# A two-layer hybrid trunk with mixture of experts on one core: a fourth 64-slot expert item, state-space input products over a 96-row stack, and a first-phase ring of six slots

## The chip, the cores and the metric

The kernel runs on 1 core of one Trainium2 chip. The metric is the device time of one execution in microseconds (us), lower is better. Five engines work side by side: TensorE (PE, with its weight loads as PEld), VectorE (DVE), ScalarE (ACT), GpSimd (POOL) and SyncE (SP), which here only issues the weight transfers. Each runs its own instructions in order and meets the others at semaphores.

## The reference: what is computed

256 tokens of width 1024 pass two layers. Each layer is a mixer and a feed-forward part; the first feed-forward is dense, the second a mixture of 8 experts with the best 2 per token. All weights are float32.

```python
def hybrid_mixer(xn, ...):
    q, k, v, u_ssm, h_conv, b_gate, c_gate, gate_logits = jnp.split(xn @ w_in, IN_SPLITS, axis=-1)
    y_a = stick_breaking_attention(q, k, v) @ w_br_a
    y_b = s5_ssm(u_ssm, ...) @ w_br_b
    y_c = short_conv(h_conv, b_gate, c_gate, conv_w) @ w_br_c
    merged = g[:, :, 0] * y_a + g[:, :, 1] * y_b + g[:, :, 2] * y_c      # g = sigmoid(gate_logits)
    return merged @ w_out
# in s5_ssm: 16 groups of 16 channels and 64 states
    bu_re = jnp.einsum('gph,blgh->blgp', bb_re, ug)
    bu_im = jnp.einsum('gph,blgh->blgp', bb_im, ug)
# the second feed-forward
    for e in range(N_EXPERTS):
        out = out + combine[..., e:e + 1] * swiglu(xn, w_gate[e], w_up[e], w_down[e])
```

Each expert has three matrices of 1024 x 3584, so the expert weights are 8 x 3 x 1024 x 3584 x 4 bytes = 352.3 MB. With the inputs that are timed, the experts 0 to 7 get 73, 59, 72, 59, 67, 72, 58 and 52 tokens.

## The kernel before

**The first phase** is both mixers and the dense feed-forward. Its weights come as units of 1 MB, in the order of the list `STREAM`, into `ring`, which has `RING` = 7 slots: unit n goes to slot n % RING. A mixer's units are q0, q1, k0, k1, v0, v1, u0, h0, b0, c0, four units gC0 to gC3, gA0, the two units brA0 and brA1, gA1 to gA3, gB0 to gB3 and wo0 to wo3; each gA unit feeds two gate steps, so steps gA6 and gA7 use unit gA3. SP issues the loads in this order (L631). Before unit n it waits until the slot is free. For most units that is when the unit n - RING has been split. The units brA are used raw, and SP waits for the end of their last user, the PE step gA7:

```python
                    old_l, old = STREAM[n - RING]
                    if old[:2] == "br":
                        sp.wait_ge(work_done, Group((old_l, "g" + old[2], KT - 1)).done)
                    else:
                        sp.wait_ge(lo_ready, SPLIT.index((old_l, old)) + 1)
```

**The split.** A unit is cut into a high part (ACT, rounded to float32r, L1235) and a low part (DVE, L1501) in `parts`, which has three places. PE multiplies three pairs of parts, each in one pass (L752), where a float32 product takes more passes. ACT and DVE split a unit when they come to the step that is `AHEAD` = 3 units before its use: the first of the two steps of a unit calls `splits.upto`, ahead of that step's own work. So at step gA6 both engines first split gB1, then do gA6.

**The order of work** on each engine is the list `STEPS`, in which the steps of attention (z, softplus, tail, attend), of the convolution (h, b, c), of the state space (bbT, u, eight steps bu, two steps ys, gelu, glu) and of the gates (gC, gA, gB) are interleaved by hand. Three banks of PSUM (`work`) go round: PE begins a group only when the bank's reader three groups before is done. A step bu multiplies 32 rows of `bbT` by 32 rows of `uT` in float32, twice (L873). Between gA7 and gB0 stands glu, whose PE product needs the output of ACT's gelu. ACT and DVE do gelu right behind gA6 and before gA7.

**The expert phase.** Items of work are (expert, slots). A full item has 96 slots (3 groups of 32), a short one 64; `FEW_AT` names the short ones, 1, 4 and 7, which go to the experts with the fewest tokens. PE's products have a stationary operand of 32 slots, four side by side (L1141 for gate and up, L1159 for down), so an item's PE time follows its groups, while its weights are always 44 MB. The weights stream through `moe_ring`, 34,816 floats per partition in the place of ring, br_slot, parts, hs and xs (17.8 MB), each load waiting (L647) until PE has used what lay there.

## Time and profile before

| what | value |
|---|---|
| three runs | 1540.42, 1537.77, 1540.18 us; median 1540.18 |
| profiled execution, its own time | 1538.63 us |
| its span, first to last instruction | 1536.9 us |
| outside the span | 1.73 us |
| busy: PE, DVE, ACT, POOL | 1502.9, 599.6, 347.7, 219.5 us |
| moved from memory | 462 MB |
| mean granted clock | 0.994 |

The three runs spread over 2.65 us (0.17%). The table's busy times are over the whole span; the phases have different limits, and what an edit is worth has to be read in its own phase.

### The profile page before, as it was taken

The page shows a single profiled execution, that of the slowest core. Times are in us where ns is not written, and L with a number is a line of the kernel's source. Part 1 is how long each engine was busy: PE and PEld are TensorE (multiplying, and loading weights), DVE is VectorE, ACT ScalarE, POOL GpSimd, SP SyncE. Part 2 cuts the span into 40 slices and gives each one's busy share as a digit, 9 for nine tenths or more (in the row PEclk, how much of TensorE's full clock was granted, in tenths as well). Part 3 has the DMA queues.
Part 4 walks back from the last instruction along what each step waited for, and adds up shares of the span by engine and source line. Part 5 has one row for each costly group of instructions (what it writes and reads, how often), then busy time and mean ns, then how long its engine had stood idle before and what let it go on. Part 6 is the DMA issues. An engine that isn't in the chain of part 4 may idle for free.

```text
span 1536.9 us, 30324 instructions
## 1 busy us (share of the span) xinstructions
PE 1502.9 (98%) x13463; PEld 922.1 (60%) x13463; DVE 599.6 (39%) x925; ACT 347.7 (23%) x427; POOL 219.5 (14%) x283
## 2 busy tenths in 40 slices
PE   7999999999999999999999999999999999999997
PEld 6988999999999988994333333333333323333331
DVE  6888667755556477564111211211202012011021
ACT  5443355444445453331000000000000000000001
POOL 3447369300000137200000000000000000000000
PEclk9999999999999999999999999999999999999998
DMA  9732395554554522589999999999999999999995
GB/s 275 234 110 83 116 282 166 191 192 165 192 192 151 174 88 83 165 325 385 372 392 419 419 419 419 419 419 420 419 419 420 420 418 419 419 419 420 419 419 222
DMA packets 146339, 465.00 MB, mean 303 GB/s; under 512 B 10144, under 2 KB 92064, under 8 KB 131872
## 3 DMA queue, kind: packets, MB, share of 16 engines
q1 hardware_dynamic: 143296, 461.40, 77.7%
q8 instruction: 106, 1.74, 0.5%
q0 software_dynamic: 416, 1.05, 0.3%
q10 hardware_dynamic: 2496, 0.61, 0.3%
q14 instruction: 25, 0.20, 0.0%
HBM read 461.98 MB, written 1.05 MB: 301 GB/s over the span
## 4 chain that ended last, share of the span: by engine, by line
PE 59%; DMA 5%; SPq 3%; ACT 1%; DVE 1%; issue 0%; POOL 0%; DVEq 0%; ACTq 0%; POOLq 0%
PE work L1141 14%; PE acc L1159 13%; PE work L752 11%; PE acc L1141 11%; PE ssm_y L1141 4%; SPq L647 3%; DMA moe_ring<-in_moe_w_down 2%; DMA moe_ring<-in_moe_w_gate 2%; DMA moe_ring<-in_moe_w_up 2%; PE acc L1096 1%; PE acc L1109 1%; PE work L873 0%; PE acc L752 0%; PE acc L843 0%; PE work L779 0%
## 5 line engine op out<-in xcount | busy, mean ns | idle before, releaser
L752 PE MATMUL work<-xs,parts 128*128 128x256 f32 x3600 | 455.3, 287 | 9.7 <-DVE xs L1508 4.8
L752 PEld LDWEIGHTS work<-xs,parts 128*128 128x128 f32 x3600 | 442.2, 193 | 19.7 <-issue 15.7
L1141 PE MATMUL work<-moe_ring,arena 128*32 128x448 f32 x2688 | 276.1, 539 | 0.1
L1501 DVE TENSOR_TENSOR parts<-ring,parts 128x2048 fp32r<-128x2048 f32 x94 | 220.0, 2345 | 121.8 <-ACT parts L1235 121.7
L1159 PE MATMUL acc<-moe_ring,arena 128*32 128x512 f32 x2352 | 257.6, 593 | 8.6 <-DMA moe_ring<-in_moe_w_down 7.0
L1141 PE MATMUL acc<-moe_ring,arena 128*32 128x448 f32 x2048 | 216.5, 540 | 1.0 <-ACT arena L1421 0.8
L1235 ACT ACTIVATE parts<-ring 128x2048 fp32r<-128x2048 f32 x94 | 178.7, 1907 | 89.3 <-PE work L752 62.6
L1159 PEld LDWEIGHTS acc<-moe_ring,arena 128*32 128x32 f32 x2352 | 75.8, 110 | 186.2 <-issue 167.9
L1141 PEld LDWEIGHTS work<-moe_ring,arena 128*32 128x32 f32 x2688 | 87.3, 110 | 165.7 <-issue 160.7
L1908 DVE TENSOR_TENSOR arena<-arena,work 128x448 f32<-128x448 f32 x42 | 23.7, 616 | 347.9 <-ACT arena L1421 347.9
L1421 ACT ACTIVATE arena<-acc 128x448 f32<-128x448 f32 x32 | 15.7, 541 | 633.5 <-PE work L1141 633.5
L1141 PEld LDWEIGHTS acc<-moe_ring,arena 128*32 128x32 f32 x2048 | 64.0, 110 | 129.7 <-issue 123.4
L752 PE MATMUL acc<-hs,parts 128*128 128x256 f32 x672 | 83.0, 283 | 1.0 <-DVE hs L1733 1.0
L752 PEld LDWEIGHTS acc<-hs,parts 128*128 128x128 f32 x672 | 81.6, 192 | 1.1 <-DVE parts L1501 1.1
L1141 PE MATMUL ssm_y<-moe_ring,arena 128*32 128x448 f32 x640 | 74.8, 539 | 0.0
L1892 DVE SCALAR_TENSOR_TENSOR arena<-acc,arena 128x512 f32<-128x512 f32 x28 | 21.0, 751 | 108.8 <-PE acc L1096 107.3
L2004 POOL TENSOR_SCALAR_AFFINE_SELECT arena<-arena 128x512 f32<-128x512 f32 x16 | 19.6, 1227 | 296.7 <-DVE arena L1640 273.4
L1341 ACT ACTIVATE sig<-work 128x256 f32<-128x256 f32 x48 | 18.4, 383 | 123.3 <-PE work L752 123.3
L1917 DVE STREAM_TRANSPOSE arena<-acc 128x768 f32<-128x768 f32 x8 | 7.9, 983 | 97.1 <-PE acc L1114 97.1
L1141 PEld LDWEIGHTS ssm_y<-moe_ring,arena 128*32 128x32 f32 x640 | 20.9, 110 | 39.2 <-issue 39.2
L1931 DVE TENSOR_TENSOR arena<-arena,acc 64x512 f32<-64x512 f32 x5 | 3.4, 679 | 92.7 <-ACT arena L1439 92.7
L2092 POOL TENSOR_TENSOR arena<-arena 128x256 f32<-128x256 f32 x16 | 31.2, 1947 | 45.0 <-DVE arena L1676 45.0
(312 smaller groups left out, 1060.3 us busy)
## 6 DMA issues: line engine op xcount, KB each, us to landing
moe_ring<-in_moe_w_gate SPq DMA_DIRECT2D x128, 896.0 KB, 23.8
moe_ring<-in_moe_w_up SPq DMA_DIRECT2D x128, 896.0 KB, 23.7
moe_ring<-in_moe_w_down SPq DMA_DIRECT2D x112, 1024.0 KB, 25.2
ring<-in_w_in SPq DMA_DIRECT2D x44, 1024.0 KB, 6.5
ring<-in_dense_w_gate SPq DMA_DIRECT2D x14, 1024.0 KB, 5.3
ring<-in_dense_w_up SPq DMA_DIRECT2D x14, 1024.0 KB, 5.1
ring<-in_dense_w_down SPq DMA_DIRECT2D x14, 1024.0 KB, 4.9
ring<-in_w_out SPq DMA_DIRECT2D x8, 1024.0 KB, 13.0
```

The lines of the kernel that those rows point to most:

```text
L647: sp.dma_start(moe_view(n, u), w).then_inc(moe_full[sem_of(n, u)], 16)
L752: last = nc.tensor.matmul(out_ap, a, b, start=start and n == 0, stop=stop and n == len(pairs) - 1, skip_group_check=shared)
L1141: last = nc.tensor.matmul(banks[g][GRP * q:GRP * q + GRP, 0:CHUNK], x, w[:, q * CHUNK:q * CHUNK + CHUNK], start=k == 0, stop=k == KT - 1, ...
L1159: last = nc.tensor.matmul(acc[GRP * q:GRP * q + GRP, b, :], eh[:, which, 2 * u + kk, g * GRP:g * GRP + GRP], w[:, kk, half * OUT_COLS:half ...
L1235: nc.scalar.activation(parts[:, s % PARTS, 0, :], ring[:, n % RING, :], ACT.Copy)\
L1341: nc.scalar.activation(sig[:, n % 2, :], bank[:, 0:L], ACT.Sigmoid).then_inc(sig_ready, 1)
L1421: nc.scalar.activation(esilu[:, g, :], gate_banks[g][:, 0:CHUNK], ACT.Silu).then_inc(silu_set, 1)
L1501: tt(parts[:, s % PARTS, 1, :], ring[:, n % RING, :], parts[:, s % PARTS, 0, :].bitcast(F32), ALU.subtract).then_inc(lo_ready, 1)
L1892: stt(h_tok[:, t, lo:lo + OUT_COLS], acc[:, half, :], own_share[:, t:t + 1], h_tok[:, t, lo:lo + OUT_COLS], ALU.mult, ALU.add).then_inc(ad ...
L1908: tt(erow[:, g * CHUNK:(g + 1) * CHUNK], esilu[:, g, :], up_banks[g][:, 0:CHUNK], ALU.mult)\
L2004: last = nc.gpsimd.affine_select(out=blk, in_=blk, compare_op=ALU.is_gt, fill=0.0, base=0, pattern=[[0, HB], [1, P]], channel_multiplier=-1)
L2092: tt(rtmp[:, 0, :], s_re, cosT[:, t, :], ALU.mult)
```

## The change

There are three edits. `FEW_AT` gets a fourth short item, now 1, 3, 5 and 7. The ring of the first phase loses one slot. In the slot's place stands `b_stack`: `bb` and `u` are each cut into a high and a low part, twelve small transfers each per layer stack them in 96 rows (high, high, low against high, low, high), and one float32r product over 96 rows replaces the float32 product over 32. Parts lie in the buffers of h and b of the convolution (`b_high`, `b_low`), in `u_high` (in bbT's place) and in `sig` (`u_low`), so ACT waits for the transfers before it writes there. The first loads of the expert weights are ordered by when their place comes free.

```diff
-    FEW_AT = (1, 4, NE - 1)
+    FEW_AT = (1, 3, 5, NE - 1)
...
-    RING = 7
+    RING = 6
     PARTS = 3
+    STACK = 3
     BR_AT = RING * UW
-    PARTS_AT = BR_AT + UW
+    BB_AT = BR_AT + UW
+    PARTS_AT = BB_AT + UW
...
+            b_stack = before_experts.enter_context(nc.sbuf_tensor("b_stack", [P, SJ, 2, P], F32R))
...
-        bbT = sb("bbT", [P, 4, P])
+        u_high = sb("u_high", [P, CT * L])
...
+        STACKED = 16 * STACK * (P // 32)
...
+            def stack_b(l):
+                sp.wait_ge(b_low_ready, l + 1)
+                for block, part in enumerate((b_high, b_high, b_low)):
+                    for m in range(P // 32):
+                        to = b_stack[rows_of(block), :, :, :].rearrange("r (a m) c n -> r m a (c n)", m=P // 32)
+                        sp.dma_start(to[:, m, :, :].bitcast(F32),
+                                     part[rows_of(m), :].rearrange("r (a n) -> r a n", n=2 * P)).then_inc(b_stacked, 16)
...
             for n, (l, name) in enumerate(STREAM):
                 if n == 1:
                     sp.wait_ge(params_loaded, 16 * PARAMS)
+                if n - RING == STREAM.index((l, "u0")) + 1:
+                    stack_b(l)
+                if n - RING == STREAM.index((l, "u0")) + 3:
+                    stack_u(l)
...
-            for s in range(5):
-                first_of_ring(s)
...
+            for s in sorted(range(FIRST_TURN), key=lambda s: (free_after(s)[-1][0], s)):
+                for _, signal, value in free_after(s):
+                    sp.wait_ge(signal, value)
                 load_unit(*UNITS[s], 0, True)
...
                     elif kind == "bu":
                         if t == 0:
-                            pe.wait_ge(bbT_ready, l + 1)
-                            pe.wait_ge(u_ready, l + 1)
-                        a, b = t // 4, 32 * (t % 4)
+                            pe.wait_ge(b_stacked, STACKED * (l + 1))
+                            pe.wait_ge(u_stacked, STACKED * (l + 1))
                         for q in range(2):
-                            last = nc.tensor.matmul(bank[:, q * L:q * L + L], bbT[b:b + 32, 2 * q + a, :],
-                                                    uT[b:b + 32, a, :], start=True, stop=True)
+                            last = nc.tensor.matmul(bank[:, q * L:q * L + L], b_stack[0:32 * STACK, t, q, :],
+                                                    u_stack[0:32 * STACK, t, :], start=True, stop=True)
...
                     elif kind in ("h", "b"):
                         bank = arrived(Group((l, kind, t)))
+                        act.wait_ge(b_stacked, STACKED * (l + 1))
...
                     elif kind == "bbT":
                         bank = arrived(Group((l, kind, t)))
-                        nc.scalar.activation(bbT[:, :, :].rearrange("p t n -> p (t n)"), bank[:, :], ACT.Copy)\
-                            .then_inc(bbT_ready, 1)
+                        nc.scalar.activation(b_high.bitcast(F32R), bank[:, :], ACT.Copy).then_inc(b_high_ready, 1)
+                    elif kind == "u":
+                        bank = arrived(Group((l, kind, t)))
+                        nc.scalar.activation(u_high[:, :].bitcast(F32R), bank[:, :], ACT.Copy).then_inc(u_high_ready, 1)
...
+                        dve.wait_ge(u_high_ready, l + 1)
+                        tt(u_low.bitcast(F32R), bank[:, :], u_high[:, :], ALU.subtract).then_inc(u_low_ready, 1)
...
+                    elif kind == "bbT":
+                        bank = arrived(Group((l, kind, t)))
+                        dve.wait_ge(b_high_ready, l + 1)
+                        tt(b_low.bitcast(F32R), bank[:, :], b_high, ALU.subtract).then_inc(b_low_ready, 1)
```

SP's instructions in the first mixer, before the change. The names are buffer, source and shape; in brackets stand the semaphores that SP waits for (`lo_ready` counts split units, `work_done` PE's finished groups).

```order
L618 DMA br_slot<-in_w_br_c 128x2x1024
L631 DMA ring<-in_w_in 128x8x256 [waits lo_ready] x5
L631 DMA ring<-in_w_br_a 128x2x1024 [waits lo_ready] x2
L631 DMA ring<-in_w_in 128x8x256 [waits lo_ready] x3
L618 DMA br_slot<-in_w_br_b 128x2x1024 [waits work_done]
L631 DMA ring<-in_w_in 128x8x256 [waits lo_ready] x2
L631 DMA ring<-in_w_in 128x8x256 [waits work_done] x2
L631 DMA ring<-in_w_out 128x8x256 [waits lo_ready] x4
```

The same place on SP with the change:

```order
L654 DMA br_slot<-in_w_br_c 128x2x1024
L667 DMA ring<-in_w_in 128x8x256 [waits lo_ready] x3
L630 DMA b_stack<-arena 32x2x256 [waits b_low_ready]
L630 DMA b_stack<-arena 32x2x256 x11
L667 DMA ring<-in_w_in 128x8x256 [waits lo_ready] x2
L638 DMA hs<-u_high 32x2x256 [waits u_low_ready]
...
L667 DMA ring<-in_w_br_a 128x2x1024 [waits lo_ready] x2
L667 DMA ring<-in_w_in 128x8x256 [waits lo_ready] x3
L654 DMA br_slot<-in_w_br_b 128x2x1024 [waits work_done]
L667 DMA ring<-in_w_in 128x8x256 [waits lo_ready]
L667 DMA ring<-in_w_in 128x8x256 [waits work_done] x2
L667 DMA ring<-in_w_in 128x8x256 [waits lo_ready]
```

Behind the load of w_br_b stood two loads (gB0, gB1) that wait for a split and then two (gB2, gB3) that wait for PE's gA7. With six slots only gB0 is left ahead of that wait, and the two behind it are gB1 and gB2.

ACT's instructions around gelu in the first mixer, before the change. An ACTIVATE into `parts` is the high half of a split, with the slot of the ring that it reads; `sig` is a gate step; L1326 is gelu.

```order
L1341 ACTIVATE sig<-work 128x256 [waits gate_used,work_done] x2
L1235 ACTIVATE parts<-ring 128x2048 [waits work_done,slot_full0]
L1341 ACTIVATE sig<-work 128x256 [waits gate_used,work_done]
L1326 ACT_TABLE_LOAD
L1326 ACTIVATE arena<-arena 128x256 [waits gelu_in] x2
L1341 ACT_TABLE_LOAD [waits gate_used]
L1341 ACTIVATE sig<-work 128x256 [waits work_done]
L1330 ACTIVATE arena<-work 128x512 [waits work_done]
L1235 ACTIVATE parts<-ring 128x2048 [waits work_done,slot_full1]
```

The same place with the change:

```order
L1377 ACTIVATE sig<-work 128x256 [waits gate_used,work_done] x2
L1266 ACTIVATE parts<-ring 128x2048 [waits work_done,slot_full3]
L1377 ACTIVATE sig<-work 128x256 [waits gate_used,work_done]
L1360 ACT_TABLE_LOAD
L1360 ACTIVATE arena<-arena 128x256 [waits gelu_in] x2
L1377 ACT_TABLE_LOAD [waits gate_used]
L1377 ACTIVATE sig<-work 128x256 [waits work_done]
L1364 ACTIVATE arena<-work 128x512 [waits work_done]
L1266 ACTIVATE parts<-ring 128x2048 [waits work_done,slot_full4]
```

The order on ACT stays. The unit whose split stands in front of gA6 and gelu is gB1 both times: number 21 of the stream, in slot 21 % 7 = 0 before and 21 % 6 = 3 now.

## Rows read from the trace of the kernel before

**Rows 1.** The page: busy time, and GB/s in 40 slices of the span.

```profile
PE 1502.9 (98%) x13463; PEld 922.1 (60%) x13463; DVE 599.6 (39%) x925; ACT 347.7 (23%) x427; POOL 219.5 (14%) x283
GB/s 275 234 110 83 116 282 166 191 192 165 192 192 151 174 88 83 165 325 385 372 392 419 419 419 419 419 419 420 419 419 420 420 418 419 419 419 420 419 419 222
```

**Rows 2.** Windows of the expert phase: stretch, busy PE, PEld, DVE, ACT, POOL, clock, DMA, GB/s.

```profile
780.00:800.00 20.00, 20.00 (x200) 6.37 (x196) 3.36 (x11) 0.00 (x0) 0.00 (x0) 1.00 1.01 420
...
1220.00:1240.00 20.00, 17.29 (x164) 4.40 (x156) 4.17 (x4) 1.42 (x3) 0.00 (x0) 1.00 1.01 419
...
1518.00:1521.00 3.00, 2.20 (x20) 0.58 (x24) 0.00 (x0) 0.00 (x0) 0.00 (x0) 1.00 0.47 191
```

**Rows 3.** Instruction groups of PE by line and shape in the expert phase.

```profile
L1141 PE MATMUL work<-moe_ring,arena 128*32 128x448 f32 x2688 | 276.1, 539 | 0.1
L1159 PE MATMUL acc<-moe_ring,arena 128*32 128x512 f32 x2352 | 257.6, 593 | 8.6 <-DMA moe_ring<-in_moe_w_down 7.0 <-DVE arena L1919 1.6
L1141 PE MATMUL acc<-moe_ring,arena 128*32 128x448 f32 x2048 | 216.5, 540 | 1.0 <-ACT arena L1421 0.8 <-DMA moe_ring<-in_moe_w_gate 0.3
L1141 PE MATMUL ssm_y<-moe_ring,arena 128*32 128x448 f32 x640 | 74.8, 539 | 0.0
```

**Rows 4.** Timeline of PE at a step bu: start, length, line, instructions.

```profile
139.99 1.12 PE L873 MATMUL work<-arena,bbT 32*128 32x256 f32 x4
```

**Rows 5.** Timeline of PE at glu, which begins when gA7 ends, first mixer.

```profile
177.05 1.89 PE L752 MATMUL work<-arena,wglu 128*128 128x256 f32 x8
```

**Rows 6.** Timeline of SP: the two loads that wait for gA7, first mixer.

```profile
177.25 0.99 SPq L631 DMA_DIRECT2D ring<-in_w_in  x2
```

**Rows 7.** Timeline of ACT: the split of gB1, gelu, and the split of gB2.

```profile
167.14 1.91 ACT L1235 ACTIVATE parts<-ring 128x2048 fp32r<-128x2048 f32 x1
...
173.38 0.81 ACT L1326 ACTIVATE arena<-arena 128x256 f32<-128x256 f32 x2 [0.23 <-DVE arena L1680]
...
182.53 1.91 ACT L1235 ACTIVATE parts<-ring 128x2048 fp32r<-128x2048 f32 x1 [2.96 <-DMA ring<-in_w_in]
```

**Rows 8.** Timeline of DVE: gA6, gelu's input, and the low part of gB2.

```profile
171.94 0.42 DVE L1691 TENSOR_TENSOR arena<-sig,work 128x256 f32<-128x256 f32 x1 [0.50 <-ACT sig L1341]
...
172.86 0.87 DVE L1680 SCALAR_TENSOR_TENSOR arena<-arena,dskip,ssm_y 128x256 f32<-128x256 f32 x2
...
184.48 2.29 DVE L1501 TENSOR_TENSOR parts<-ring,parts 128x2048 fp32r<-128x2048 f32 x1 [4.11 <-ACT parts L1235]
```

**Rows 9.** PE before and behind its longest wait, and the clock there (timeline, windows).

```profile
43.49 11.68 PE L752 MATMUL work<-parts,xs 128*128 128x256 f32 x96
...
71.55 14.44 PE L752 MATMUL work<-xs,parts 128*128 128x256 f32 x96 [2.69 <-DVE parts L1501]
...
76.00:78.00 2.00, 2.00 (x12) 2.00 (x12) 2.00 (x1) 0.00 (x0) 1.93 (x2) 0.59 0.53 90
```

**Rows 10.** Timeline of ACT and DVE, first mixer: splits, rotation tables, convolution.

```profile
69.40 1.90 ACT L1235 ACTIVATE parts<-ring 128x2048 fp32r<-128x2048 f32 x1
...
69.11 2.29 DVE L1501 TENSOR_TENSOR parts<-ring,parts 128x2048 fp32r<-128x2048 f32 x1
...
78.43 1.65 DVE L1602 TENSOR_TENSOR arena<-arena,power 128x1024 f32<-128x1024 f32 x1
...
81.25 1.23 DVE L1604 TENSOR_TENSOR arena<-arena,power 128x1024 f32<-128x1024 f32 x1
...
86.03 0.69 DVE L1647 TENSOR_TENSOR arena<-work,arena 128x512 f32<-128x512 f32 x1 [0.97 <-PE work L752]
...
89.62 0.69 DVE L1658 TENSOR_TENSOR arena<-arena 128x512 f32<-128x512 f32 x1
```

**Rows 11.** Timeline of PE: the branch product of gC0, and the second tail step.

```profile
92.17 1.03 PE L752 MATMUL work<-arena,br_slot 128*128 128x256 f32 x4
...
115.51 0.91 PE L843 MATMUL acc<-arena,neg_incl 128*128 128x384 f32 x2 [0.29 <-POOL arena L2004]
```

**Rows 12.** The page: SP's smallest transfers, KB each, median us to landing.

```profile
out<-arena SPq DMA_DIRECT2D x4, 256.0 KB, 2.1
```

More of the change, by code:

```diff
@@ L327, in trunk_kernel @@
         x_parts = [xs[:, q * KT * L:(q + 1) * KT * L].rearrange("p (k n) -> p k n", n=L) for q in range(2)]
+        u_stack = hs[:, :].rearrange("p (t n) -> p t n", n=L)
         h_parts = hs[:, :].rearrange("p (b q f n) -> p b q f n", b=2, q=2, n=L)
@@ L386, in trunk_kernel @@
         v_tiles = v[:, :, :].rearrange("p t n -> p (t n)").rearrange("p (t n) -> p t n", n=L)
+        flat_conv = [conv[:, :, :].rearrange("p t n -> p (t n)") for conv in (hconv, bconv)]
+        b_high, b_low = flat_conv
+        u_low = sig[:, :, :].rearrange("p t n -> p (t n)")
         scaled_pair = attn[:, :, :].rearrange("p h n -> p (h n)")[:, 0:4 * L].rearrange("p (b q n) -> p b q n", b=2, q=2)
@@ L606, in _, with rows_of, stack_u @@
                     .then_inc(x_loaded[half], 16)
+            def rows_of(m):
+                return slice(32 * m, 32 * m + 32)
+            def stack_b(l):
[5 more added lines that the diff above has]
+                                     part[rows_of(m), :].rearrange("r (a n) -> r a n", n=2 * P)).then_inc(b_stacked, 16)
+            def stack_u(l):
+                sp.wait_ge(u_low_ready, l + 1)
+                for block, part in enumerate((u_high, u_low, u_high)):
+                    for m in range(P // 32):
+                        to = u_stack[rows_of(block), :, :].rearrange("r (a m) n -> r m a n", m=P // 32)
+                        sp.dma_start(to[:, m, :, :].bitcast(F32),
+                                     part[rows_of(m), :].rearrange("r (a n) -> r a n", n=L)).then_inc(u_stacked, 16)
             for n, (l, name) in enumerate(STREAM):
@@ L657, in load_block, with free_after @@
                 return waited
-            def under(s):
+            def free_after(s):
                 lo, hi = PLACE[UNITS[s]]
-                return range(lo // UW, (hi - 1) // UW + 1)
-            def first_of_ring(s):
-                behind = max(m for m in range(RING) if (len(STREAM) + m) % RING in under(s))
-                sp.wait_ge(lo_ready, S0 + behind - RING + 1)
-                load_unit(*UNITS[s], 0, True)
-            def last_part_under(s):
-                slots = [(at - PARTS_AT // UW) // 2 for at in under(s) if PARTS_AT // UW <= at < HS_AT // UW]
-                return max((n for n in range(S0 - PARTS, S0) if n % PARTS in slots), default=-1)
@@ L672, in _ @@
-            sp.wait_ge(down_banks, KT // 2)
-            in_hs = [s for s in range(FIRST_TURN) if PLACE[UNITS[s]][0] >= HS_AT and PLACE[UNITS[s]][1] <= XS_AT]
-            for s in in_hs:
-                load_unit(*UNITS[s], 0, True)
-            for s in range(5):
-                first_of_ring(s)
-            sp.wait_ge(work_done, Group((DEPTH - 1, "gB", KT - 1)).done)
-            in_br = [s for s in range(FIRST_TURN) if BR_AT <= PLACE[UNITS[s]][0] and PLACE[UNITS[s]][1] <= PARTS_AT]
-            for s in in_br:
-                load_unit(*UNITS[s], 0, True)
@@ L682, in _, with meets @@
-            for s in range(5, HALF_UNITS):
-                first_of_ring(s)
-            for part in range(S0 - PARTS, S0):
-                sp.wait_ge(*used_up(*SPLIT[part]))
-                for s in range(HALF_UNITS, FIRST_TURN):
-                    if s not in in_hs + in_br and part == (
-                            S0 - 1 if PLACE[UNITS[s]][1] > XS_AT else last_part_under(s)):
-                        load_unit(*UNITS[s], 0, True)
+                def meets(start, size):
+                    return lo < start + size and start < hi
@@ new lines, in free_after @@
+                after = []
+                for j in range(RING):
+                    if meets((len(STREAM) - RING + j) % RING * UW, UW):
+                        split_no = S0 - RING + j
+                        after.append((split_no - PARTS + 0.8, lo_ready, split_no + 1))
+                if meets(BR_AT, UW):
+                    after.append((S0 - 5 + 0.1, work_done, Group((DEPTH - 1, "gB", KT - 1)).done))
+                if meets(BB_AT, UW) or meets(HS_AT, XS_AT - HS_AT):
+                    after.append((0, work_done, Group((DEPTH - 1, "bu", SJ - 1)).done))
@@ new lines, in free_after @@
+                for part in range(S0 - PARTS, S0):
+                    if meets(PARTS_AT + part % PARTS * 2 * UW, 2 * UW):
+                        after.append((part + 0.1, *used_up(*SPLIT[part])))
+                if meets(XS_AT, MOE_SIZE - XS_AT):
+                    after.append((S0 - 1 + 0.1, *used_up(*SPLIT[S0 - 1])))
+                return sorted(after, key=lambda entry: entry[0])
+            for s in sorted(range(FIRST_TURN), key=lambda s: (free_after(s)[-1][0], s)):
+                for _, signal, value in free_after(s):
+                    sp.wait_ge(signal, value)
+                load_unit(*UNITS[s], 0, True)
@@ L1333, in _ @@
                         n = gate_number(l, kind[1], t)
+                        if kind == "gC" and t == 0:
+                            act.wait_ge(u_stacked, STACKED * (l + 1))
                         if kind == "gB" and t >= KT - 2:
```

11 lines of the change are left out of this document (8 added, 3 removed).

## The prediction

> **What bounds the kernel now.** I read the page first. PE is busy for 1502.9 of 1536.9 us, and the slices show two regimes of transfer: 83 to 385 GB/s up to slice 20, then 419 or 420 almost to the end [rows 1]. So PE's share alone does not say who sets the end. I looked at each phase for itself.
>
> In the expert phase the windows answer it. From 780 us on the transfers run at 419 or 420 GB/s, whether PE is busy for 20.00 of 20 us or for 17.29 [rows 2]; in slices 19 to 21, which are item 0, they run at 372 to 392 [rows 1]. The weights are 352.3 MB, at 420 GB/s 839 us. PE's products of the phase take 276.1 + 216.5 + 74.8 + 257.6 = 825.0 us [rows 3]. By item: five full items have 3 groups and three short ones 2, together 21, at 825.0 / 21 = 39.3 us; a full item costs PE 118 us, a short one 79, and the transfers of any item 105. PE falls 13 us behind in a full item and makes up 26 in a short one. The ring holds 17.8 MB, 42 us of transfer, and absorbs this. The ring is full only in item 0, where PE sets the pace; behind it the transfers never stop. The expert phase is bound by transfer once item 0 is through.
>
> The first phase is the reverse: PE goes from product to product, and the transfers rest between units. There a microsecond of PE, or of a wait of PE, is a microsecond of the whole, and also of the start of the expert phase.
>
> **The short item.** Item 3 and item 5 become short and item 4 full: one group fewer, 39.3 us less PE work. Item 0 stays full and item 1 short, so the only stretch that PE paces is as it was, and from there on the bytes left and their rate are the same. What hides the edit is the stream itself: PE waits longer for weights. I cost it at 0. The four experts with the fewest tokens outside item 0's have 52, 58, 59 and 59, all within 64 slots, so no ninth item is made. The last item is short as before and PE had caught up there (2.20 busy of 3.00 us at the end, with the clock at 1.00) [rows 2], so the tail stays too.
>
> **The products.** A step bu takes 1.12 us for two float32 products in four records [rows 4]. With float32r parts it is two records at the pace of the other split products, 11.68 us for 96 or 0.12 each [rows 9]; with the tail of the last one 0.32 us, so 0.80 less. That the new ones have 96 rows and not 128 should not make them slower. 16 steps give 16 x 0.80 = 12.8 us. Two of them, bu2 in either layer, give nothing: they stand between z1 and tail1, and PE already waits 0.29 us at tail1 for the chain through ACT, DVE and POOL [rows 11]. That returns 1.6 us. Net -11.2.
>
> **The stacking, first layer.** DVE is the late engine here; PE waits for its split until 71.55 [rows 9]. At 69.11 DVE starts that split [rows 10]; now `b_low` goes first, one operation on 128x512, whose like takes 0.69 us and hides 0.1 of it [rows 10]. PE waits 0.6 us more. Then SP issues twelve copies. Two loads were issued in 0.99 us [rows 6], so twelve take 6.0, and the last lands 2.1 us later if it is like SP's stores [rows 12]: they start at 70.0, and 70.0 + 8.1 = 78.1. ACT sits at its copy of h until then, and behind it are the splits of gC0 (at 69.40 before [rows 10]) and gC1. On DVE follow the low part of gC0, three operations of rotation tables (78.43 to 82.48, 4.1 us), the low part of gC1, and the convolution (86.03 to 90.31, 4.3 us) [rows 10]. Behind 78.1 come 0.5 + 1.9 us on ACT and 2.3 + 4.1 + 2.3 + 4.3 on DVE, less 0.1 at each handover: the convolution is ready at 93.4. PE asks for it at 92.17 + 0.6 [rows 11]: it waits 0.6 us. DVE then runs some 3 us late, and the three banks pass on about 1.5 us of that to PE. Together +2.7. In the second layer there are no tables in the way and nothing is late, so the copies are covered: 0. `stack_u` has more than 10 us of h, b, c and gC0 on PE as its cover in both layers.
>
> Both ends for the copies: 0 below; above, twelve at 2.1 us each one behind the other, 25.2 us, which would make PE wait some 18 us in the first layer and, without the tables, 14 in the second. I take the low end, because SP's own issues are the nearest rows. The Trainium skill speaks against the edit here: "DMA: Bandwidth & Descriptors", section Bandwidth, puts a transfer of 64 KB at 0.95 us and calls those below that size descriptor-dominated. By it twelve copies would take 11.4 us, the total would come to about 1567, and no row here shows such copies on SP.
>
> **The ring of six.** For nearly all units a slot less costs nothing: a load is issued six units ahead of its use and a load lands within 5.3 us (177.25 to 182.53 [rows 6, 7]), while PE spends 5.8 us on a unit of 48 products [rows 9]. One place is different. The units behind brA0 and brA1 in the ring wait not for a split but for PE's gA7. With seven slots these are gB2 and gB3, issued at 177.25, when gA7 has ended at 177.05 [rows 5, 6]; gB2 is first read by ACT at 182.53, after 2.96 us of waiting, and by then gelu is done (173.38 to 174.19) [rows 7] and PE is in the gB steps. With six slots they are gB1 and gB2, and ACT and DVE split gB1 ahead of gA6, where it now happens at 167.14 [rows 7]. PE goes on to the end of gA7. Then glu needs gelu, gelu is behind gA6 on ACT and DVE, and gA6 is behind the split of a unit whose load has just been issued. The chain, with T = 177.05: load seen by ACT at T + 5.5 (182.53 [rows 7]), high part 1.9, low part done at T + 9.7 (184.48 + 2.29 [rows 8]), then gA6's product, its sum and gelu's input, 171.94 to 173.73, 1.8 us [rows 8], and gelu's end 0.46 us behind that (174.19 [rows 7]): T + 11.9. PE had glu at T [rows 5]. It stands idle for 11.9 us in each mixer, 23.8 in all; nothing on PE can cover it, because the products are issued in order.
>
> The clock follows. After 2.69 us of waiting PE ran at the lower level of 1.2 GHz (granted 0.59 as late as 76 to 78 us) and took 14.44 us for 96 products that take 11.68 at full clock [rows 9]: 2.7 us lost. A wait of 11.9 us should cost this again, so 5.4 in two layers; the bounds are 0 and, with the low level for twice as long, 11.
>
> What is late next: the gate steps of ACT behind glu start late, but PE starts glu late by the same amount, and gB2 has landed by then. The first expert loads move with the splits, and as a whole they get more time ahead of PE.
>
> **The sum.** The profiled execution took 1538.63 us: - 11.2 + 2.7 + 23.8 + 5.4 = + 20.7 gives 1559.3. The median of the three runs shown is 1.55 us above the profiled one. I say 1559.
>
> **The rivals.**
> *The wait is hidden and the kernel is faster.* If gB1 were in the ring in time, what is left is - 11.2 + 2.7: 1530. For it speaks only that a slot less is a rare limit elsewhere. It is decided by when gB1 lands: by about 167 us, where ACT splits it now [rows 7], nothing is lost, and each us behind that costs one as soon as gelu's margin of some 3 us is gone. Against it stands the order: the load waits for gA7, the split is ahead of gA6. Chance 0.06.
> *The short item pays.* If PE were the bound throughout, 39.3 us less work would come off: 1559 - 39 = 1520, or about 1540 if half does. For it speaks that PE is busy for 20.00 of 20.00 us in most windows; against it that the transfers stay at 419 GB/s when PE rests [rows 2]. Chance 0.05.
> *The copies are slow.* With 1 us each they end 6 us later, PE waits 6 us more in the first layer and about half as long in the second, where a part is covered: 1568; with 2 us, above 1580. Chance 0.12.
> *The clock falls in the starved items.* Short items would keep PE waiting a quarter of the time. If it then ran at 1.2 GHz, a short item would take 157 us against 105 of transfer, up to 52 us for each of three. Against it: 17.29 of 20 and 2.20 of 3 us busy, both at 1.00 [rows 2]. Chance 0.03.
> The forecast itself gets 0.74.
>
> **How the numbers follow.** The forecast's own range is 1553 to 1566: the stall 10 to 13 us, the clock 0 to 3 a time, the first layer's stacking 0 to 5. The range reaches down to 1550 for a part of the gain in the expert phase and up to 1569 for copies of 1 us. A change below 0.2% (3.1 us) can't be told from none here. Faster holds the first rival and most of the second, 0.10; within 0.2% 0.02; slower 0.88.
>
> **What would show it.** Right: PE idle for about 12 us ahead of glu in each mixer, with ACT waiting for a load of w_in ahead of a split; the granted clock near 0.5 behind it; bu at about 0.26 us; PE busy down by some 50 us to about 1450; transfers still at 419 GB/s and the expert phase, from its first product to the end, as long as before. Wrong: no idle ahead of glu; the expert phase shorter by more than 3 us; `b_stack` copies landing after 80 us in the first layer. The likeliest error of size is the clock's price and the copies; of sign, only the wait for gA7.

## The result, and the profile of the changed kernel

The changed kernel takes 1565.6 us (median of 4 runs, 1564.57 to 1566.6), the kernel before 1539.97 us (4 runs): a ratio of 1.0168, 95% interval 1.0156 to 1.0181. It is 25.6 us slower; the forecast was 1559, 19 slower, with a range up to 1569. The profiled execution took 1565.42 us, its span 1563.6.

The page of the kernel after, which answers to [rows 1]: busy time by engine, the granted clock of PE in 40 slices, and the transfer rate in the same slices.

```profile
PE 1467.7 (94%) x13063; PEld 906.3 (58%) x13063; DVE 606.3 (39%) x927; ACT 346.4 (22%) x426; POOL 214.2 (14%) x283
PEclk9999899999999999899999999999999999999999
GB/s 277 157 197 74 138 189 166 195 165 192 183 189 135 167 225 55 145 233 364 381 370 420 419 419 419 420 419 419 419 420 419 419 420 419 420 419 419 419 420 232
```

PE is busy for 35.2 us less, yet the span is 26.7 us longer: what was saved in work came back as idle time. Its clock dips in slices 4 and 16 (the first is 0), in which the two glu steps lie. The transfers run at 419 or 420 GB/s from slice 21 on, as before.

The waits of the kernel after: engine and line that waited, engine and line that released it, us in total, times, longest.

```profile
ACT parts L1266 <- DMA ring<-in_w_in: 31.8, 2, 15.9
...
PE work L784 <- ACT arena L1360: 24.0, 2, 12.0
```

L1266 is ACT's split, L1360 gelu. Two waits of ACT for a load, two of PE for gelu; neither line had a wait of this size before. The timeline of SP, ACT, DVE and PE (one below the other) shows how they hang together in the first mixer.

```profile
178.61 2.46 SPq L667 DMA_DIRECT2D ring<-in_w_in  x3
...
183.95 1.91 ACT L1266 ACTIVATE parts<-ring 128x2048 fp32r<-128x2048 f32 x1 [15.87 <-DMA ring<-in_w_in]
...
189.59 0.81 ACT L1360 ACTIVATE arena<-arena 128x256 f32<-128x256 f32 x2 [2.16 <-DVE arena L1722]
...
185.96 2.29 DVE L1537 TENSOR_TENSOR parts<-ring,parts 128x2048 fp32r<-128x2048 f32 x1 [16.18 <-ACT parts L1266]
...
189.08 0.87 DVE L1722 SCALAR_TENSOR_TENSOR arena<-arena,dskip,ssm_y 128x256 f32<-128x256 f32 x2
...
176.69 1.89 PE L784 MATMUL work<-arena,ring 128*128 128x256 f32 x8
190.55 3.75 PE L784 MATMUL work<-arena,wglu 128*128 128x256 f32 x8 [11.97 <-ACT arena L1360]
193.74 3.42 PE L784 MATMUL work<-xs,parts 128*128 128x256 f32 x24
```

The rows show a circle in time: PE ends gA7 at 178.6, only then does SP load gB1; ACT has stood at its split of gB1 for 15.87 us, DVE behind ACT for 16.18, and gelu (189.59) is queued on both behind that split. PE, which has nothing but glu next, stands idle for 11.97 us. Then it runs at half speed: glu takes 3.75 us against 1.89 [rows 5]. The windows there (columns as in [rows 2]) show the clock, idle first, then at work:

```profile
182.00:184.00 2.00, 0.00 (x0) 0.00 (x0) 0.00 (x0) 0.05 (x1) 0.00 (x0) 0.98 1.08 364
...
190.00:192.00 2.00, 1.45 (x4) 1.21 (x5) 0.00 (x0) 1.97 (x4) 0.00 (x0) 0.50 1.11 350
...
194.00:196.00 2.00, 2.00 (x17) 1.91 (x16) 0.69 (x1) 1.67 (x2) 0.97 (x1) 0.96 1.10 349
```

PE stopped at 178.6, the granted clock was at 0.50 from 184 on and back at 0.96 in the stretch from 194. In the second mixer the same happens: glu starts at 658.90, behind 11.99 us of idle time.

The second cost is the stacking of the first mixer. The timeline of SP, of ACT, and of PE at the first gC branch (compare [rows 10, 11]):

```profile
71.50 8.96 SPq L630 DMA_DIRECT2D b_stack<-arena  x12
...
81.97 0.60 ACT L1339 ACTIVATE arena<-work 128x512 f32<-128x512 f32 x1 [13.18 <-DMA b_stack<-arena]
...
97.14 1.13 PE L784 MATMUL work<-arena,br_slot 128*128 128x256 f32 x4 [3.76 <-DVE arena L1700]
...
98.36 4.54 PE L784 MATMUL work<-xs,parts 128*128 128x256 f32 x24
```

SP issued the twelve copies in 8.96 us, 0.75 us each. ACT's copy of h waited for them for 13.18 us, the convolution (L1700) was late behind it, PE waited 3.76 us and then ran slowly (4.54 us for 24 products that take 3.04 to 3.14 at full clock). ACT went on at 81.97 us, so the last copy had landed only then: this is one of the prediction's own signs of being wrong, copies into `b_stack` landing after 80 us.

**Where the time stands in all kernels.** The start of a kernel varies from one execution to the next: the first tail step begins between 83.9 and 87.1 us in the twelve traces, in no order that follows the edits. So I read each trace in two stretches: from PE's first tail step to its first expert product, and from there to the end of the span. Each number is the difference of two starts in PE's timeline.

| kernel | first phase, us | against before | expert phase, us | median, us |
|---|---|---|---|---|
| before | 613.6 | | 837.5 | 1540.0 |
| after | 639.2 | +25.7 | 837.5 | 1565.6 |
| e1_order | 613.5 | -0.1 | 837.2 | 1539.3 |
| e2_float32_products | 645.6 | +32.0 | 835.9 | 1570.3 |
| e3_short_items | 613.5 | 0.0 | 836.2 | 1537.2 |
| e4_filled | 633.5 | +19.9 | 836.5 | 1559.2 |
| e5_room | 609.6 | -3.9 | 837.7 | 1534.6 |
| e6_splits_behind | 602.6 | -11.0 | 837.4 | 1528.5 |
| e7_splits_behind_before | 613.9 | +0.3 | 837.1 | 1538.6 |
| e8_later_split | 610.8 | -2.8 | 837.1 | 1536.2 |
| e9_items_back | 602.6 | -10.9 | 838.2 | 1528.0 |
| e10_tail_later | 611.3 | -2.3 | 837.7 | 1534.5 |

The kernel before, run again beside the experiments, had medians of 1538.97 (e1 to e4), 1538.3 (e5 to e8) and 1538.38 us (e9, e10), 1.0 to 1.7 us below the 1539.97 beside the kernel after. Where two runs from different groups are compared below, the stretches of the table or the ratios are the safer numbers. The expert phase is within 1.6 us of the kernel before in every kernel, with three or four short items, begun at 688 or at 733 us, and with either order of the first expert loads. That order, the third edit, was not run by itself. All that follows is about the first phase.

### The profile page after: what moved, and what is told of

It is laid out like the page before. It is cut to its first block, busy times and chain, and to the rows that moved or that the text cites. A ratio compares the mean times of both kernels' runs of the same rounds, so it can differ in the third digit from the quotient of the medians.

```text
span 1563.6 us, 29591 instructions
## 1 busy us (share of the span) xinstructions
PE 1467.7 (94%) x13063; PEld 906.3 (58%) x13063; DVE 606.3 (39%) x927; ACT 346.4 (22%) x426; POOL 214.2 (14%) x283
## 3 DMA queue, kind: packets, MB, share of 16 engines
q0 software_dynamic: 416, 1.05, 0.3%
HBM read 461.98 MB, written 1.05 MB: 296 GB/s over the span
## 4 chain that ended last, share of the span: by engine, by line
PE 41%; DMA 15%; SPq 7%; DVE 2%; POOL 1%; issue 1%; ACT 1%; DVEq 0%; ACTq 0%; POOLq 0%
PE work L1172 10%; PE acc L1190 9%; PE work L784 8%; PE acc L1172 7%; DMA moe_ring<-in_moe_w_down 7%; SPq L683 7%; DMA moe_ring<-in_moe_w_up 5%; DMA moe_ring<-in_moe_w_gate 3%; PE ssm_y L1172 2%; PE acc L1127 1%; PE acc L1140 1%; POOL arena L2134 0%; PE acc L784 0%; DVE parts L1537 0%; DMA ring<-in_w_in 0%
## 5 line engine op out<-in xcount | busy, mean ns | idle before, releaser
L1190 PE MATMUL acc<-moe_ring,arena 128*32 128x512 f32 x2240 | 249.8, 594 | 23.8 <-DMA moe_ring<-in_moe_w_down 22.0
L1172 PE MATMUL work<-moe_ring,arena 128*32 128x448 f32 x2560 | 264.7, 540 | 7.3 <-DMA moe_ring<-in_moe_w_up 7.2
L1266 ACT ACTIVATE parts<-ring 128x2048 fp32r<-128x2048 f32 x94 | 179.0, 1908 | 111.9 <-PE work L784 60.3
L1190 PEld LDWEIGHTS acc<-moe_ring,arena 128*32 128x32 f32 x2240 | 71.6, 110 | 198.4 <-issue 146.9
L1172 PEld LDWEIGHTS work<-moe_ring,arena 128*32 128x32 f32 x2560 | 82.5, 110 | 169.0 <-issue 140.0
L1172 PEld LDWEIGHTS acc<-moe_ring,arena 128*32 128x32 f32 x2048 | 63.4, 110 | 136.0 <-issue 114.2
L1172 PE MATMUL ssm_y<-moe_ring,arena 128*32 128x448 f32 x512 | 60.1, 539 | 0.0
L1172 PEld LDWEIGHTS ssm_y<-moe_ring,arena 128*32 128x32 f32 x512 | 17.2, 110 | 30.9 <-issue 30.9
L1953 DVE STREAM_TRANSPOSE arena<-arena 128x1344 f32<-128x1344 f32 (+1 forms) x16 | 33.7, 2109 | 0.6
## 6 DMA issues: line engine op xcount, KB each, us to landing
moe_ring<-in_moe_w_down SPq DMA_DIRECT2D x112, 1024.0 KB, 25.7
```

The costliest lines, as they stand in the source:

```text
L1172: last = nc.tensor.matmul(banks[g][GRP * q:GRP * q + GRP, 0:CHUNK], x, w[:, q * CHUNK:q * CHUNK + CHUNK], start=k == 0, stop=k == KT - 1, ...
L1190: last = nc.tensor.matmul(acc[GRP * q:GRP * q + GRP, b, :], eh[:, which, 2 * u + kk, g * GRP:g * GRP + GRP], w[:, kk, half * OUT_COLS:half ...
L1266: nc.scalar.activation(parts[:, s % PARTS, 0, :], ring[:, n % RING, :], ACT.Copy)\
L1953: nc.vector.transpose(eh[:, which, :, :].rearrange("p f (g n) -> p f g n", g=NG)[:, :, 0:ng, :], erow[:, :].rearrange("p (g i f) -> p f g ...
```

## The experiments

**The wait for gB1.** In e1_order one line of the order of loads differs from the kernel after; no compute engine has an instruction moved.

```diff
-    + ["gA0"] + [f"brA{n}" for n in range(QW // UC)] + [f"gA{n}" for n in range(1, GU)]
+    + ["gA0", "gA1"] + [f"brA{n}" for n in range(QW // UC)] + [f"gA{n}" for n in range(2, GU)]
```

> The kernel after, with one edit to the order of loads: gA1 stands ahead of brA0 and brA1, so that the two slots that are held until gA7 pass to gB2 and gB3, as they did with seven slots. The instructions of PE, ACT, DVE and POOL are the same. Theory (the wait for gB1 costs the time): both waits of 12.0 us ahead of glu and the slow stretches behind them (1.8 and 1.5 us) go, 27.3 in all: 1565.6 - 27.3 = 1538.3, no idle of PE ahead of glu over 0.5 us. Rival (six slots are too few in general, or brA is now late for gA0): PE waits elsewhere in its place, and the time stays above 1548.

Measured 1539.33 us, ratio to before 1.0003 (0.9993 to 1.0012). No wait ahead of glu is left; 25.7 us of the first phase came back by moving one load. Six slots are enough in this order. That the kernel is no faster than before, though its products are shorter, has its reason in new waits: 3.43 us at the first gC branch (with slow products behind it), 1.0 us more at the second tail step of each mixer, 0.84 us at the first ys step, and 2.56 and 2.58 us at the last ys step. PE's timeline in the second mixer, then POOL's and DVE's beside it:

```profile
622.75 1.89 PE L784 MATMUL work<-arena,ring 128*128 128x256 f32 x8
627.22 1.07 PE L911 MATMUL ssm_y<-arena,cblk 128*32 128x256 f32 x16 [2.58 <-POOL arena L2139]
...
618.34 2.64 POOL L2134 TENSOR_TENSOR arena<-arena 128x256 f32<-128x256 f32 x1 [1.28 <-DVE arena L1718]
620.94 0.92 POOL L2135 TENSOR_TENSOR arena<-arena 128x256 f32<-128x256 f32 x1
621.82 0.96 POOL L2136 TENSOR_TENSOR arena<-arena 128x256 f32<-128x256 f32 x1
622.73 2.77 POOL L2137 TENSOR_TENSOR arena<-arena 128x256 f32<-128x256 f32 x1
...
618.12 2.26 DVE L1537 TENSOR_TENSOR parts<-ring,parts 128x2048 fp32r<-128x2048 f32 x1
...
622.37 2.56 DVE L1537 TENSOR_TENSOR parts<-ring,parts 128x2048 fp32r<-128x2048 f32 x1 [0.19 <-ACT parts L1266]
```

POOL's two long operations begin inside DVE's two splits and end 0.6 us behind them; the same operations beside other work take 0.72 to 1.01 us. In this trace twelve of POOL's 128x256 operations take 2.64 us or more: every one begins inside a split and ends 0.57 to 0.61 us behind its end. A short operation is held in the same way, as POOL's and DVE's rows in the kernel after show (its neighbours of the same shape take 0.20 to 0.27 us):

```profile
239.09 2.17 POOL L2094 TENSOR_TENSOR power<-power 128x8 f32<-128x8 f32 x1
...
238.91 2.29 DVE L1537 TENSOR_TENSOR parts<-ring,parts 128x2048 fp32r<-128x2048 f32 x1 [0.53 <-ACT parts L1266]
```

So what a collision costs POOL is what is left of DVE's split when POOL's operation begins, whatever that operation's own size. The Trainium skill says it of the pair ("GPSIMD Engine Reference", Specifications): POOL's way to SBUF is shared with DVE and contended when DVE reads two inputs from SBUF, as this split does. The trace agrees, at 1.9 and 2.0 us for these two.

In e2_float32_products the state-space products of the kernel before are put back; the ring keeps six slots, and the items and the order of the expert loads stay as in the kernel after.

```diff
-    pe.wait_ge(b_stacked, STACKED * (l + 1))
-    pe.wait_ge(u_stacked, STACKED * (l + 1))
+    pe.wait_ge(bbT_ready, l + 1)
+    pe.wait_ge(u_ready, l + 1)
...
-    b_stack[0:32 * STACK, t, q, :], u_stack[0:32 * STACK, t, :]
+    bbT[b:b + 32, 2 * q + a, :], uT[b:b + 32, a, :]
```

> The kernel after with the state-space products as they were before: float32 products, no split of b and u, no copies; the 2048 floats of b_stack stay unused, so that the ring still has six slots. Theory (ring of six alone makes the loss): 1540.0 + 27.3 = 1567.3, PE idle 12 us ahead of glu in both layers. Rival (the stack with its copies makes the loss, the ring costs nothing): about 1540.

Measured 1570.33 us, ratio 1.0201 (1.0186 to 1.0217). PE's timeline at glu in both mixers:

```profile
190.94 3.75 PE L755 MATMUL work<-arena,wglu 128*128 128x256 f32 x8 [12.46 <-ACT arena L1329]
...
664.59 3.75 PE L755 MATMUL work<-arena,wglu 128*128 128x256 f32 x8 [11.95 <-ACT arena L1329]
667.78 3.95 PE L755 MATMUL work<-xs,parts 128*128 128x256 f32 x24
```

The ring of six alone makes the loss, and a larger one than that of the whole change: +32.0 us in the first phase against +25.7. The rival, that the copies make it, falls. The stack was worth 6.3 us beside the stall; beside e1_order's free run it was worth nothing. Most of the difference is the finding above: while DVE waits for gB1 it makes no split beside POOL, and the last ys step waits only 0.47 us in both mixers (641.05 in the second of the kernel after) instead of 2.56 and 2.58, 4.2 us together. Another 1.5 us is e2's own: its stall and the slow stretches behind glu are longer by that much.

In e8_later_split the load is as late as in the kernel after, but the split stands elsewhere.

```diff
-    while self.next < min(SPLIT.index((l, name)) + AHEAD, S0):
+    while self.next < min(SPLIT.index((l, name)) + AHEAD - late, S0):
...
-    splits.upto(l, unit_of(kind, t))
+    splits.upto(l, unit_of(kind, t), (kind, t) in (("gA", 6), ("gB", 0)))
```

> The kernel after, with the order of loads as it is (gB1's load still waits for PE's gA7), but ACT and DVE split gB1 at step gB0 and not at step gA6, so that gelu is no longer behind that load. Theory (it is the place of the split ahead of gelu that costs 12 us, not the late load): the wait ahead of glu goes; the low part of gB1 is ready some 10 us behind the end of gA7, PE asks for it some 9 us behind: 1 to 2 us a layer are left, 1539.3 + 3 = about 1542. Rival (PE needs gB1 as soon as gelu, so the wait only moves to gB1): 5 us or more a layer are left, above 1550.

Measured 1536.2 us, ratio 0.9989 (0.998 to 0.9998), better than the 1542 expected. PE's timeline, and ACT's split of gB1:

```profile
177.33 1.89 PE L784 MATMUL work<-arena,wglu 128*128 128x256 f32 x8
...
187.28 2.99 PE L784 MATMUL work<-xs,parts 128*128 128x256 f32 x23 [0.58 <-DVE parts L1537]
...
182.89 1.92 ACT L1266 ACTIVATE parts<-ring 128x2048 fp32r<-128x2048 f32 x1 [3.04 <-DMA ring<-in_w_in]
```

With the load still issued at 177.5, when gA7 has ended, PE waits 0.58 us at gB1 (0.53 in the second mixer) and not 12. So the 12 us need both the late load and the split's place in two engines' queues, ahead of gelu; e1_order took away the one, this kernel the other, and either ends the wait. The rest of the surprise is again POOL: the last ys step waits 0.43 and 0.45 us.

**The clock.** In e4_filled PE works through the wait.

```diff
     pe.wait_ge(glu_loaded, 16 * (l + 1))
+    w = weights(l, "gB0")
+    for n in range(96):
+        nc.tensor.matmul(bank[:, 0:L], w[0][:, n % KT, 0:P], x_parts[0][:, n % KT, :], start=True, stop=True)
     pe.wait_ge(gelu_out, CT * (l + 1))
```

> The kernel after with 96 float32r products of 128x128 by 128x256, whose result is overwritten, issued by PE ahead of its wait for gelu in each glu step. They fill about 11.7 of the 12.0 us in which PE stood idle. Theory (the slow stretch behind the wait comes from the idle time): the wait for gelu ends at the same time, but PE runs at 2.4 GHz behind it: 1.8 and 1.5 us less, 1565.6 - 3.3 = 1562.3. Rival (the clock falls for another reason, or the price is paid elsewhere): 1565.6 or, if the products reach beyond the wait, more.

Measured 1559.23 us, ratio 1.0138 (1.0123 to 1.0154): 5.8 us less in the first phase than the kernel after. PE's timeline:

```profile
176.93 11.86 PE L920 MATMUL work<-xs,parts 128*128 128x256 f32 x96
189.14 1.99 PE L784 MATMUL work<-arena,wglu 128*128 128x256 f32 x8 [0.35 <-ACT arena L1364]
190.78 3.22 PE L784 MATMUL work<-xs,parts 128*128 128x256 f32 x24
193.84 1.03 PE L784 MATMUL work<-arena,br_slot 128*128 128x256 f32 x4
```

From glu to the first gB branch it is 4.70 us here and 6.45 in the kernel after (190.55 to 197.00), in the second mixer 4.71 and 6.10. That is 3.1 us, where 3.3 were expected, and the granted clock stays at 1.00 from 176 to 198 us: PE slowed down because it had been idle. Of the other 2.6 us, 1.7 lie between the first gB branch and the root mean square of the dense part, where the kernel after and e2 have a wait of 1.3 us for DVE's sum of squares and this kernel has none. In the kernel after DVE's last three operations of that sum take 2.45 us (from 252.87), beside POOL's 128x256 operations on the tables of the second mixer; here they take 1.48 us (from 248.58), beside shorter ones. This suggests the two engines in each other's way once more, and no run tests it.

**The short items.** In e3_short_items the kernel before gets the new items and nothing else.

```diff
-    FEW_AT = (1, 4, NE - 1)
+    FEW_AT = (1, 3, 5, NE - 1)
```

> The kernel before with four items of 64 slots in place of three (items 1, 3, 5 and 7 in place of 1, 4 and 7) and nothing else. Theory (the expert phase behind item 0 goes at the pace of the transfers): 1540.0, within 1.5 us, with PE busy for some 39 us less and transfers at 419 GB/s. First rival (PE is the bound of the phase): 39 us less, 1501, or 1520 if half does. Second rival (the clock falls where PE waits for weights): above 1545.

Measured 1537.24 us, ratio 0.9989 (0.998 to 0.9998). The page has PE busy for 1478.3 us, 24.6 less and not 39; the expert products alone are 368 fewer and 33.5 us shorter (791.5 against 825.0 [rows 3]). The rate is 418 to 420 GB/s from slice 21 on, as the theory had it. A gain of 1.7 us is at the edge of what the runs can tell, and far from 39 or 20.

In e9_items_back the fastest kernel below goes back to the three items (the same line, reversed).

> The kernel e6_splits_behind with the items of 64 slots as before (1, 4 and 7 in place of 1, 3, 5 and 7): one group of 39.3 us more of PE's work. Theory (transfers set the pace behind item 0, whenever it begins): the time of e6_splits_behind, 1528.5, within 2 us. Rival (with the first phase shorter, PE is the bound for a part of the phase): 3 us or more above it.

Measured 1528.03 us, ratio 0.993 (0.9916 to 0.9943), beside 1528.52 with four short items. So the edit is worth nothing there, and the 1.7 us of e3 are not confirmed.

**The copies.** In e5_room, built on e1_order, the parts of b lie elsewhere, and ACT's copy of h need not wait.

```diff
-    b_high, b_low = flat_conv
+    b_high, b_low = [sring[:, n, :, :].rearrange("p c n -> p (c n)") for n in range(2)]
...
-    act.wait_ge(b_stacked, STACKED * (l + 1))
     dst = hconv if kind == "h" else bconv
```

> The kernel e1_order (loads in the order gA0, gA1, brA0, brA1) with the parts of b kept in the first two places of the ring of states, which are free until the first product bu, in place of the convolution's buffers. ACT's copy of h no longer waits for the twelve copies into b_stack. Theory (the copies cost 3.4 us, through ACT's copy of h and the convolution, in the first layer only): PE's wait of 3.43 us ahead of the first gC branch goes, 1539.3 - 3.4 = 1535.9. Rival (DVE is full there, with or without the copies): the wait stays above 2 us, and the time within 1 us of 1539.3.

Measured 1534.6 us, ratio 0.9981 (0.9972 to 0.999), 3.8 less in the first phase than e1_order. PE comes to the first gC branch without a wait (92.73). The copies, as many and nearly as slow (8.49 us), then cost PE no wait at the gC branch; it was the borrowed buffer that carried that cost.

**POOL beside DVE's splits.** In e6_splits_behind, built on e5_room, DVE makes the low parts of gB0 and gB1 behind gelu's input.

```diff
-    if unit_of(kind, t) is not None:
+    if unit_of(kind, t) is not None and (kind, t) not in (("gA", 4), ("gA", 6)):
         splits.upto(l, unit_of(kind, t))
...
             stt(uT[:, a, :], uT[:, a, :], dskip[:, l, a:a + 1], ssm_y[:, a, :], ALU.mult, ALU.add)\
                 .then_inc(gelu_in, 1)
+        splits.upto(l, "gA3")
```

> The kernel e5_room with one more edit on DVE alone: the low parts of gB0 and gB1 are made behind gelu's input and not ahead of gA4 and gA6. In e1_order POOL's operations on a state take 2.6 to 2.8 us beside such a split and 0.7 to 0.9 otherwise, and PE waits 2.56 and 2.58 us for POOL's last state. Theory (these waits are POOL slowed by DVE's splits): they fall to under 0.5 us in both layers, some 5 us less than e5_room: 1531. Rival (DVE's own work, 8 steps of 5.2 us beside the gates, sets the end of the last state): under 1 us less. Second rival (the splits are then late for gB0): PE waits 2 to 4 us at gB0 in their place, no gain or a loss.

Measured 1528.52 us, ratio 0.994 (0.9927 to 0.9954): 6.1 less than e5_room and 9.8 below the kernel before; with e9_items_back it is the fastest of all. POOL's operations on the last state, PE's step ys, and DVE's two splits:

```profile
611.70 0.73 POOL L2133 TENSOR_TENSOR arena<-arena 128x256 f32<-128x256 f32 x1 [1.27 <-DVE arena L1716]
...
614.77 0.81 POOL L2137 TENSOR_TENSOR arena<-arena 128x256 f32<-128x256 f32 x1
...
617.95 1.07 PE L910 MATMUL ssm_y<-arena,cblk 128*32 128x256 f32 x16
...
620.28 4.49 DVE L1535 TENSOR_TENSOR parts<-ring,parts 128x2048 fp32r<-128x2048 f32 x2
```

On this state no operation of POOL is long any more. Its six take 4.7 us from first start to last end, and 8.8 in e5_room (615.75 to 624.58), where both splits stand behind the state's scan in DVE's queue as well and so cannot have delayed its start; PE does not wait at this ys step. On an earlier state one is still held by a split, for 2.79 us (598.38), and costs PE nothing. The moved splits are ready at 624.8, ahead of the first gB product at 625.19.

In e7_splits_behind_before the same edit is made on the kernel before.

> The kernel before with that edit on DVE alone (low parts of gB0 and gB1 behind gelu's input). PE does not wait for a state there in the kernel before, so the theory gives no change: 1540 within 1.5 us. If the order of splits were a gain of its own, apart from the products, it would be 2 to 5 us below.

Measured 1538.63 us, ratio 1.0003 (0.9994 to 1.0012). With the slower products PE arrives at ys late enough. This order of splits is worth something only with the faster products.

**What is left at tail1.** In e10_tail_later, built on e6_splits_behind, the second tail step of a mixer (tail1) stands one gate step later.

```diff
-    if t == 4:
+    if t == 5:
         STEPS.append(("tail", 1))
```

> The kernel e6_splits_behind with the second tail of each mixer one gate step later (behind gC5 and not gC4) on all engines. In e6_splits_behind PE waits 1.54 and 1.31 us at tail1 for the chain through ACT, DVE and POOL. Theory (the wait is slack that can be had by order): both waits go, 1528.5 - 2.8 = 1525.7. Rival (the next link, attend behind POOL's mask, is then late by as much): 1528.5, with a wait at attend; or, with z1's chain now colliding with bu on DVE, more.

Measured 1534.48 us, ratio 0.9971 (0.9958 to 0.9983), 6 us slower than e6. The rival was right in its second form, with more than 1528.5. PE's timeline at attend in the two mixers:

```profile
131.88 0.83 PE L887 MATMUL acc<-arena 128*64 128x256 f32 x4 [3.17 <-POOL arena L2045]
...
586.38 1.13 PE L887 MATMUL acc<-arena 128*64 128x256 f32 x4 [2.81 <-POOL arena L2045]
```

The wait of 1.54 and 1.31 us at tail1 became one of 3.17 and 2.81 us at the next link, 3.1 us more. PE also has 2.6 us of waits for DVE at the convolution and the bu steps of the gC stretch that e6_splits_behind has not; together they are about the 6 us.

## Why the prediction was right, and where its sizes were off

**The ring of six** was right in place, cause and size: 11.97 and 11.99 us against 11.9, by the chain of steps as it was worked out. (From the last ys step to glu the stretch is longer by 12.13 and 12.15 us.) e1, e2 and e8 each show a part of it: the order of loads, the ring alone, the place of the split.

**The clock behind the wait** was put at 2.7 us a time, from the slow stretch of [rows 9]. It measured 1.85 and 1.50 (the time from glu to the first gB branch, 6.45 and 6.10 us, against 4.60 before, where that branch starts at 181.65 and glu at 177.05 [rows 5]), and filling the wait gave back 1.75 and 1.39. PE was back at full speed sooner than after the shorter wait in the rows of before. One wait was a thin ground for a price: at that same place e7_splits_behind_before has a wait of 2.74 us and its 96 products take 11.75, and e10_tail_later 3.29 and 11.74, with the granted clock at 1.00 all through. How long PE rested does not by itself give the cost here.

**The products** were put at 0.80 us a step. Three steps lie between the first gC branch and tail1 of the second mixer; that stretch went from 23.33 to 21.52 us though its wait grew by 1.02, so 2.83 / 3 = 0.94 a step. PE's timeline of the kernel before at the first of these steps shows the missing part, and that of e6_splits_behind beside it:

```profile
548.81 1.03 PE L752 MATMUL work<-arena,br_slot 128*128 128x256 f32 x4
549.77 1.13 PE L873 MATMUL work<-arena,bbT 32*128 32x256 f32 x4
550.82 3.14 PE L752 MATMUL work<-xs,parts 128*128 128x256 f32 x24
```

```profile
559.71 1.03 PE L783 MATMUL work<-arena,br_slot 128*128 128x256 f32 x4
560.39 0.59 PE L903 MATMUL work<-hs,b_stack 96*128 96x256 f32 x2
560.81 3.03 PE L783 MATMUL work<-xs,parts 128*128 128x256 f32 x24
```

From start to start the product went from 1.05 to 0.42 us, less than the forecast had it; but the branch products ahead of it, which are float32 in both kernels, are followed after 0.68 us and not after 0.96. The 32 rows are not what makes the gap: the attend products, float32 over 128 rows, start 0.96 us behind the next branch too (553.80, 554.76). So a float32 product also costs something ahead of itself, which the forecast left out. What the forecast missed most is how little of 16 x 0.94 = 15 us arrives: it had PE give back 0.8 us a mixer at tail1, the kernel after gives back 2.1 in the first and 2.3 in the second (there 1.02 more at tail1, 0.84 and 0.47 at ys), and e1_order 4.4 in the second. That the net of 10.6 us comes so near to the 11.2 of the sum is luck: a gain put too low and a loss put too low. e5, e6 and e7 show that this was order, not work: with the order mended and the room of e5_room, the products and their stack gain 11.0 us.

**The stacking of the first mixer** was put at 2.7 us. The first gC branch is 3.9 us late against the first tail step, and the slow gate step behind it costs 1.4 more. The term that was too small is the issue of a copy, taken as 0.5 us from loads of another kind; it was 0.75, so twelve took 3.0 us more. They also began at 71.50 and not at 70.0, 1.05 us of which is the later start of this execution, and landed sooner behind the last issue (1.5 us, not 2.1): ACT went on at 81.97 and not at 78.1. The rival of slow copies, at 1 us each, was half true. The Trainium skill ("DMA: Bandwidth & Descriptors", Bandwidth) gives 0.95 us for 64 KB, measured there on loads from HBM. The trace has 0.75 us from one issue to the next, between that and the forecast's 0.5. The 0.6 us more at the first split are there too (3.42 against 2.69 us), but the 96 products behind it took 13.23 us and not 14.44. e5 shows which wait carried the cost.

**Left out** were 2.9 us in and ahead of the dense part (the wait of 1.3 us for the sum of squares and smaller ones), and 1.05 us at the start, which is within the scatter. The sum also began at the profiled execution's 1538.63, 1.3 us below the median of all four runs. From the first tail step on, the terms are, in the first mixer up to ys1, products and stacking +0.3; in the second -5.2; the stalls 12.13 + 12.15; the clock 3.35; the dense part 2.9: together 25.6, against 25.7 in the table. The forecast's terms come to 20.7: stacking and the dense part were too low by 2.6 and 2.9, and the clock, too high by 2.0, hid a part of it. (In the second mixer the last ys step of the kernel after starts at 641.05.)

**The expert phase** was right: 837.5 us before and after, 835.9 to 838.2 in all twelve traces. Two smaller signs were missed: PE's busy time was to fall to about 1450 us and fell to 1467.7 (the expert products are 33.4 us shorter, not 39.3; the slow stretches take some back; the rest is not traced), and a step bu was to take 0.26 us and shows 0.59, though the next product starts 0.42 us behind it.

**The chances** were set with little for faster, 0.10. The rival "the wait is hidden" was decided where the text said it would be, at the order of load, gA7 and split; e1 shows what it would have given, and that is 1539, not the 1530 of its sum, because of POOL and of the copies.

## What to carry to other kernels

When a ring of buffers gets a slot less, look not at how many units it holds but at which unit inherits a slot with an unusually late last reader, and at what is queued behind that unit's first reader on each engine. A faster product moves PE nearer to every chain beside it: follow the nearest ones (here scan, POOL, ys) before counting the gain, and mend their order with it. Here the products alone (e1_order) and the order of splits alone (e7) gave nothing, and both with a buffer of their own for the copies gave 0.6%. Buffers borrowed for a short copy chain an engine that has no part in it to the copy's queue.

## What the runs showed of the hardware that I had not expected

- POOL's operation on 128x256 takes 0.73 us alone and 2.64 to 2.78 us when it begins inside a DVE operation of 128x2048 with both inputs in SBUF; it then ends 0.57 to 0.61 us behind DVE's, and one of 128x8 (0.20 us) took 2.17. DVE's own took 2.26 us with POOL's beginning behind it (618.12, 618.34), and 2.56 and 2.70 where one of POOL's was already running (622.37, 604.49 in e1_order).
- Behind the float32 branch products a float32 product starts 0.28 us later than a float32r product in its place (0.96 against 0.68 us).
- PE idle for 12 us, from 178.6 to 190.55: the granted clock was still 0.98 from 182 to 184, 0.50 (1.2 GHz) from 184 to 194, and 0.96 from 194 to 196. Waits of 2.7 us cost 2.7 us in three traces (before, e2, e3) and nothing in a fourth (e7).
- SP issued its copies of 32 rows from SBUF to SBUF (64 KB each) every 0.70 to 0.75 us, loads of 1 MB every 0.5 us [rows 6].
